# Gate, up and value products by token instead of by feature, and the last two down slabs of each network in token halves

## The reference

```python
def swiglu(h, w_gate, w_up, w_down):
    return (jax.nn.silu(h @ w_gate) * (h @ w_up)) @ w_down
...
for i in range(DEPTH):
    g = norm_gains[i]
    f = swiglu_2(rmsnorm_2(h, g[0]), ffn_gate[i, 0], ffn_up[i, 0], ffn_down[i, 0])
    h = h + MACARON * rmsnorm_2(f, g[1])
    mix = hybrid_mixer(rmsnorm_2(h, g[2]), cos_m, sin_m, cos_d, sin_d, w_in[i], q_norm[i], ...)
    h = h + rmsnorm_2(mix, g[3])
    f = swiglu_2(rmsnorm_2(h, g[4]), ffn_gate[i, 1], ffn_up[i, 1], ffn_down[i, 1])
    h = h + MACARON * rmsnorm_2(f, g[5])
    gate = jax.nn.sigmoid(rmsnorm_2(h, g[6]) @ w_ple_gate[i])
    h = h + rmsnorm_2((p[i].astype(h.dtype) @ w_ple[i]) * gate, g[7])
```

## Time and profile before

| | |
|---|---|
| median of 3 runs | 1837.92 us (1836.95 to 1840.16) |
| the profiled execution | 1842.03 us, its span 1840.4 us |
| mean granted TensorE clock | 0.973 |
| TensorE busy | 1734.6 us, 94% |
| weight loads | 1595.6 us, 87% |
| VectorE busy | 1216.6 us, 66% |
| ScalarE busy | 896.8 us, 49% |
| GpSimd busy | 122.2 us, 7% |
| chain that ended last | TensorE 78%, VectorE 11%, ScalarE 4% |
| transferred | 353.79 MB, 192 GB/s |

### The profile page before, as it was taken

The page is one execution under the profiler, slowest core; times in us unless marked ns, Lnnn a source line. Parts: engine busy times, 40 slices in busy tenths (PEclk is TensorE's granted clock), DMA queues, the critical chain, the costliest instruction groups (busy, mean ns, idle before and its releaser), DMA issues.

```text
span 1840.4 us, 29946 instructions
## 1 busy us (share of the span) xinstructions
PE 1734.6 (94%) x11826; PEld 1595.6 (87%) x11826; DVE 1216.6 (66%) x1599; ACT 896.8 (49%) x1235; POOL 122.2 (7%) x163
## 2 busy tenths in 40 slices
PE   6987899999899999999998999988999999999996
PEld 4986799989799998999896899978999896799986
DVE  7889787777765546555676665556655676765556
ACT  4572433356544335434476544345433557644345
POOL 2023111111010000000011000000000003000000
PEclk9998899999999999999999999998999999999999
DMA  9775598868345453555340555434555532355551
GB/s 380 280 292 182 209 358 315 308 232 312 144 172 206 182 183 134 199 193 189 136 178 10 184 200 187 177 138 148 196 193 182 172 138 69 126 184 185 180 197 42
DMA packets 61924, 353.79 MB, mean 192 GB/s; under 512 B 6522, under 2 KB 9738, under 8 KB 27792
## 3 DMA queue, kind: packets, MB, share of 16 engines
q1 hardware_dynamic: 40064, 281.24, 42.2%
q0 software_dynamic: 18384, 66.66, 10.1%
q10 hardware_dynamic: 3392, 4.72, 0.8%
HBM read 349.45 MB, written 3.15 MB: 192 GB/s over the span
## 4 chain that ended last, share of the span: by engine, by line
PE 78%; DVE 11%; ACT 4%; issue 3%; DMA 3%; POOL 0%; DVEq 0%; ACTq 0%; POOLq 0%
PE bank L528 23%; PE bank L529 23%; PE bank L530 23%; DVE w_lo L1509 2%; ACT w_hi L1021 2%; PE bank L560 1%; PE bank L562 1%; PE bank L561 1%; DMA shared<-in_mods 1%; PE bank L700 1%; DVE shared L1530 1%; PE bank L721 1%; DVE shared L2046 1%; PE bank L710 1%; DVE x L2055 1%
## 5 line engine op out<-in xcount | busy, mean ns | idle before, releaser
L528 PE MATMUL bank<-a_hi,w_hi 128*128 128x256 f32 x2648 | 758.8, 287 | 11.0 <-DVE a_lo L1577 3.6
L529 PE MATMUL bank<-a_lo,w_hi 128*128 128x256 f32 x2648 | 754.6, 285 | 0.0
L530 PE MATMUL bank<-a_hi,w_lo 128*128 128x256 f32 x2648 | 754.5, 285 | 0.0
L528 PEld LDWEIGHTS bank<-a_hi,w_hi 128*128 128x128 f32 x2648 | 513.9, 194 | 17.8 <-issue 11.5
L529 PEld LDWEIGHTS bank<-a_lo,w_hi 128*128 128x128 f32 x2648 | 514.0, 194 | 2.9 <-issue 0.7
L530 PEld LDWEIGHTS bank<-a_hi,w_lo 128*128 128x128 f32 x2648 | 513.5, 194 | 0.0
L1771 DVE TENSOR_TENSOR w_lo<-raw,w_hi 128x2048 fp32r<-128x2048 f32 x144 | 330.0, 2292 | 258.2 <-ACT w_hi L1162 258.2
L1162 ACT CAST w_hi<-raw 128x2048 fp32r<-128x2048 f32 x144 | 273.9, 1903 | 268.9 <-PE bank L530 268.9
L1509 DVE TENSOR_TENSOR w_lo<-raw,w_hi 128x2048 fp32r<-128x2048 f32 x119 | 272.1, 2292 | 133.5 <-ACT w_hi L1021 133.4
L1021 ACT CAST w_hi<-raw 128x2048 fp32r<-128x2048 f32 x122 | 231.3, 1907 | 90.9 <-PE bank L530 84.4
L528 PE MATMUL bank<-w_hi,hid_hi 128*128 128x512 f32 x548 | 215.8, 394 | 4.8 <-DVE hid_lo L2192 3.0
(11 more groups left out here) (242 smaller groups left out, 1948.8 us busy)
## 6 DMA issues: line engine op xcount, KB each, us to landing
raw<-in_stream SPq DMA_DIRECT2D x266, 1024.0 KB, 4.8
shared<-in_mods POOLq DMA_DIRECT2D x102, 512.0 KB, 6.3
grow<-in_rows POOLq DMA_DIRECT2D x12, 512.0 KB, 4.0
work<-in_mods POOLq DMA_DIRECT2D x8, 512.0 KB, 9.7
bias_rows<-work ACTq DMA_DIRECT2D x1, 2048.0 KB, 19.0
x<-in_x_t SPq DMA_DIRECT2D x1, 1024.0 KB, 6.2
x<-in_x_d ACTq DMA_DIRECT2D x1, 1024.0 KB, 4.9
work<-bias_rows ACTq DMA_DIRECT2D x1, 1024.0 KB, 10.5
```

The costliest lines, as they stand in the source:

```text
L528: pe.matmul(out, w_h, v_h, start=start, stop=False, skip_group_check=True)
L529: pe.matmul(out, w_h, v_l, start=False, stop=False, skip_group_check=True)
L530: return pe.matmul(out, w_l, v_h, start=False, stop=stop, skip_group_check=True)
```

## The change

- Gate and up columns of a group now lie side by side (512 columns), and a slab is half of the contraction (`split_rows`). `wide_slab` holds the activations of 128 tokens stationary and moves 512 weight columns. The output, by token, is gate and up of 256 features for 128 tokens in one bank. The dilated values, the shared values and the embedding gates have the same form.
- `hid` is now by token and is transposed on TensorE (`turn_hid`, four transposes a group) between the two halves of the next pair. ScalarE and VectorE read the transposed bank for `hid_hi` and `hid_lo`. The root mean square is now a scale per partition, so that the row for it and the separate scaling of gate and up are gone; `mean_row` is left for the mixers alone.
- The last two down slabs of a network run as (9, p0), the transposes of hid 10, (9, p1), (10, p0 and p1), (9, p2 and p3), (10, p2 and p3). The next stage begins with the first tokens (`first_tokens`), and `token_pair` transposes the second tokens' pieces within its second slab. `post`, `add_gated`, `turned_hi` and `turned_low` run in pieces of 128 tokens by four chunks, with the conversions of the next slabs between them.
- In FFN0 all four last modulation steps of VectorE stand ahead of the last `hidden`, and the reduction for the shared keys stands inside the last down slabs.
- In the mixer the value slabs come first, then the six others; in the shared keys and values too. Of the embedding, two gate slabs come first, then the embedding, then two gate slabs.

```diff
+            def wide_slab(slot, out, t, k, at=None, between={}):
+                for c in range(4):
+                    if at is not None:
+                        pe.wait_ge(nl_ready, at + CH * t + 4 * k + c + 1)
+                    mm = product(out[:, :], tokens(a_hi, 4 * k + c, t), tokens(a_lo, 4 * k + c, t), *weights(slot, 512 * c, 512),
+                                 start=(k == 0 and c == 0), stop=(k == 1 and c == 3))
+                    if c in between:
+                        between[c]()
                 return mm
...
+            def turn_piece(src, ready, p):
                 t, h = p // 2, p % 2
                 pe.wait_ge(*ready(p))
-                if free is not None:
-                    pe.wait_ge(*free)
-                for c in range(4 * h, 4 * h + 4):
-                    mm = pe.transpose(bank[4 + c // 2][:, (c % 2) * S + t * P:(c % 2) * S + (t + 1) * P],
-                                      src[:, t, c * P:(c + 1) * P], ident[:, :])
-                    if t == 1 and c % 2:
-                        mm.then_inc(turned, 1)
-            def turn_x(u, src, ready):
-                for p in range(4):
-                    turn_piece(src, ready, p, (f_ready, 4 * u + 4) if p == 1 else None)
+                for c in range(4):
+                    mm = pe.transpose(bank[4 + p][:, c * P:(c + 1) * P], src[:, t, (4 * h + c) * P:(4 * h + c + 1) * P], ident[:, :])
+                mm.then_inc(turned, 1)
+            def first_tokens(src, ready, warm=0, b=1):
+                keep_warm(warm, b)
+                for p in range(2):
+                    turn_piece(src, ready, p)
+            def token_pair(s, outs, at, src, ready):
+                need_slab(s)
+                wide_slab(s, outs[0], 0, 0, at)
+                need_slab(s + 1)
+                wide_slab(s + 1, outs[0], 0, 1, at, {1: lambda: turn_piece(src, ready, 2), 3: lambda: turn_piece(src, ready, 3)}).then_inc(half_done, 1)
+                wide_slab(s, outs[1], 1, 0, at).then_inc(slab_done, 1)
+                wide_slab(s + 1, outs[1], 1, 1, at).then_inc(slab_done, 1)
...
+                def first_half(done, slot, par, free=None):
+                    pe.wait_ge(lo_ready, done)
+                    if free is not None:
+                        pe.wait_ge(hl_ready, free)
+                    wide_slab(slot, bank[2 * par], 0, 0)
+                    wide_slab(slot, bank[2 * par + 1], 1, 0).then_inc(slab_done, 1)
+                def second_half(done, slot, par):
+                    pe.wait_ge(lo_ready, done)
+                    wide_slab(slot, bank[2 * par], 0, 1).then_inc(half_done, 1)
+                    wide_slab(slot, bank[2 * par + 1], 1, 1).then_inc(slab_done, 1)
+                def turn_hid(par, done):
+                    for t in range(2):
+                        pe.wait_ge(hid_done, done + (t + 1))
+                        for k in range(2):
+                            mm = pe.transpose(bank[2 * par][:, k * S + t * P:k * S + (t + 1) * P], hid[:, par, t * S + k * P:t * S + (k + 1) * P], ident[:, :])
+                        mm.then_inc(hid_turned, 1)
...
+                first_half(b + 3 * j, b + 3 * j - 1, 0, j - 1 + f0)
+                turn_hid(1, 2 * (f0 + j - 1))
+                second_half(b + 3 * j + 1, b + 3 * j, 0)
+                down(j - 1, b + 3 * j + 2, b + 3 * j + 1, 1, pieces=(0,))
+                turn_hid(0, 2 * (f0 + j))
+                down(j - 1, b + 3 * j + 2, b + 3 * j + 1, 1, pieces=(1,))
+                down(j, b + 3 * j + 3, b + 3 * j + 2, 0, last=True, pieces=(0, 1))
+                if i == 0:
+                    mod_reduce(G_KV, 3)
+                down(j - 1, b + 3 * j + 2, b + 3 * j + 1, 1, pieces=(2, 3)).then_inc(slab_done, 1)
+                down(j, b + 3 * j + 3, b + 3 * j + 2, 0, last=True, pieces=(2, 3)).then_inc(slab_done, 1)
...
-                need_slab(b + 1)
-                slab_pair((b, b + 1), (bank[0], bank[1]), before(APPLY_CHUNKS, apply2(l, LA_PREMIX)))
-                mean_row(4 * l + 1)
-                for i in range(2, 8):
-                    need_slab(b + i)
-                    if i in (4, 5, 6, 7):
+                token_pair(b, (bank[2], bank[3]), before(APPLY_CHUNKS, apply2(l, LA_PREMIX)), x, residual(u2(l, 0)))
+                mean_row(l)
+                for i in range(6):
+                    need_slab(b + 2 + i)
+                    if i in (2, 3):
+                        pe.wait_ge(qkv_act, c0 + i - 1)
+                    if i in (4, 5):
                         pe.wait_ge(qkv_dve, d0 + i - 3)
-                    if i < 6:
-                        mm = feature_slab(b + i, bank[i % 4])
-                    else:
-                        mm = token_slab(b + i, bank[i % 4])
-                    mm.then_inc(slab_done, 1)
+                    feature_slab(b + 2 + i, bank[i % 4]).then_inc(slab_done, 1)
+                    if i == 3:
+                        norm_stat(norm2(l, L_QLAT))
                     if i == 4:
-                        norm_stat(norm2(l, L_QLAT))
-                    if i == 5:
                         norm_stat(norm2(l, L_KVLAT))
...
+                post(u, 4 + 3 * l, b - 1, gain2(l, 2), b)
                 pre_squares(u)
                 c0, d0 = 8 + 8 * l, 6 * l
-                split_to(b + 3)
                 pre_rsqrt(4 * l + 1)
-                split_to(b + 4)
-                pre_row_copy(4 * l + 1)
-                def values(i):
-                    for t in range(2):
-                        ins = act.activation(v_dil[:, t, 256 * i:256 * (i + 1)], bank[2 + i][:, 256 * t:256 * (t + 1)], ACT.Copy,
-                                             scale=pre_r[:, t:t + 1])
-                    ins.then_inc(qkv_act, 1)
+                act.wait_ge(rpre_ready, 4 * l + 2)
+                act.wait_ge(rows_zero, 4)
+                for t in range(2):
+                    if t:
+                        act.wait_ge(slab_done, b + 2)
+                    else:
+                        act.wait_ge(half_done, halves_ffn(3 + 2 * l))
+                    act.activation(v_dil[:, t, :], bank[2 + t][:, :], ACT.Copy, scale=pre_r[:, t:t + 1]).then_inc(qkv_act, 1)
+                    split_to(b + 4)
+                pre_row_copy(l)
+                split_to(b + 5)
...
-                act.wait_ge(rows_zero, 4)
-                act.wait_ge(slab_done, b + 7)
-                act.wait_ge(rpre_ready, 4 * l + 2)
-                values(0)
-                act.wait_ge(slab_done, b + 8)
-                values(1)
...
-                made[0] = b + 3 * (FJ - 2) + 5
+                made[0] = b + 3 * FJ
                 j = FJ - 1
-                gate(j, j % 2, b + 3 * j)
-                split_to(b + 3 * j + 3)
-                hidden(j, j % 2, b + 3 * j + 1)
                 if i == 0:
                     mod(G_A1, 6)
-                split_to(b + 3 * j + 4)
-                hidden_lo(j, j % 2)
-                if i == 0:
                     mod(G_A1, 7)
-                split_to(b + 3 * j + 5)
+                hidden(j, 0)
+                split_to(b + 3 * FJ + 1)
+                hidden_lo(j, 0)
...
+                gained(0)
+                gained(1)
+                add(0)
+                gained(2)
+                turned_low(ap, 0, gain)
+                split_to(b + 2)
+                gained(3)
+                turned_low(ap, 1, gain)
+                add(1)
+                turned_low(ap, 2, gain)
+                turned_low(ap, 3, gain)
+                split_to(b + 3)
...
+                warm_up()
+                piece(0)
+                piece(1)
+                split_to(b + 2)
+                piece(2)
+                turned_hi(u, 0, gain)
+                piece(3)
+                for p in range(1, 4):
+                    turned_hi(u, p, gain)
+                split_to(b + 3)
...
+def split_rows(w):
+    yield wide(w[0:512])
+    yield wide(w[512:1024])
```

720 lines of the change are left out of this document (348 added, 372 removed).

## The result

| | before | changed |
|---|---|---|
| median of 4 runs each | 1839.04 us (1836.95 to 1843.09) | 1867.63 us (1862.3 to 1873.05) |
| profiled execution, its span | 1842.03, 1840.4 | 1862.3, 1860.6 |
| mean granted clock in it | 0.973 | 0.976 |
| TensorE busy | 1734.6, 94% | 1711.3, 92% |

The changed kernel takes 1.0146 times as long (95% interval 1.0120 to 1.0172): 27 us more by this ratio, 28.6 between the two medians. The forecast was 14 more, 1852 with a range from 1829 to 1868: the sign was right, the size was about half of what was measured. The profiled execution took 1862.3 against a forecast of 1856, the median is 1867.6 against 1852.

The account below looks back on a forecast made before the run. TensorE was taken to bound the kernel, busy 1734.6 of 1840.4 us. Gains of -20.8, new waits of +12.2 (FFN0) and +17.8 (mixers) and +5 for the clock gave +14: 1852 by the median, range 1829 to 1868.

Parts of the forecast that it names:

- FFN0's end: At FFN0's last hid, modulation steps awaiting transfers stand ahead of hidden: TensorE waits 10.1 us, hand-over +12.2, clock +2.
- mixers, with their clock: Ahead of the latent's up-projection, a small slab covers the rotated chain: 7.5 us wait, +8.9 per layer, clock +1.5 each.
- E + 3.2: 3.2 us after E, the end of a network's last gate/up product; at FFN0, when the loop's four modulation steps end.
- The wait at (10, p0): At a network's end, hid's low part stands behind the next slab's low part on VectorE: a new stall of 2.2 us.
- The clock term of +5: Granted clock falls after the new long waits: +2 us at FFN0, +1.5 per mixer; ends 0 and +15.
- Rival 3: At most hand-overs the clock falls, through short waits and transposes: +10 to +15 us, 1865; chance 0.15.
- I take -1.9 and -3.2: Bodies of the two modulated networks: no squares at the start, and idle TensorE the new order can hide.
- 31.9, so -0.85: Hand-over from the second network, one wait longer than the others: 31.9 us against 32.75.
- 1: The mixer's wait ahead of the up-projection does not appear, its chain having slack: 1831 us, faster; chance 0.2.
- 2: FFN0's wait is small, transfers being issued earlier, while the mixer's is there: 1842 us; chance 0.16.
- 4: In each step the wide product gains less or transposes cost more: 0.3 us per step, 66 steps, +20, 1872; chance 0.06.
- 5: VectorE's list decides, hand-overs stay as long as before and only the added waits remain: +17 us, 1869; chance 0.05.

Follow-up runs that it names:

- e10: Changed kernel with FFN0's last four modulation steps on VectorE moved from ahead of hidden to behind hid_lo; a single execution, 1860.3 us.
- e4: Changed kernel with the key latent's root and low part ahead of the mixer's last rotation, up-projection into free banks; median 1859.4 us, ratio 1.0122.
- e9: Changed kernel with 30 small filler matmuls, result unused, ahead of the wait for the key latent in the mixer; 1869.1 us.
- e3: Changed kernel with the last hid's high and low parts made ahead of the next slab's conversion; median 1857.6 us, ratio 1.0106.
- e13: Changed kernel unedited, profiled again; 1867.2 us at a mean granted clock of 0.973.
- e14: Changed kernel unedited, profiled once more; 1869.6 us at a mean granted clock of 0.970.
- e6: Changed kernel with the second network's rotary angle behind the slab conversion and hid_lo, and hid's high part ahead of the sine; median 1863.3 us.
- e11: Changed kernel with the last two down slabs in the old order, all pieces of one, then all of the other; 1850.2 us, ratio 1.0071.
- e15: Changed kernel without the ten filler matmuls after the second network; that hand-over took 43.90 us instead of 45.95.
- e16: Changed kernel with the edits of e10, e3, e4 and e6, without the filler after the second network; that hand-over took 41.93 us instead of 43.94.
- e12: Changed kernel with the edits of e10, e3, e4 and e6, and the last two down slabs in the old order; 1825.6 us, ratio 0.9943.

## Why the prediction was right or wrong

Forecast and measured, profile against profile, in us (measured: stages of the table above and of the earlier trace rows):

| term | forecast | measured |
|---|---|---|
| bodies of six networks | -5.1 | -4.8 |
| three hand-overs (mixers, FFN1's) | -4.85 | -1.9 |
| four after mixers and outputs | -10.4 | -8.6 |
| embedding, to the gates' end | +3.2 | +4.1 |
| behind the gates, and the last part | -3.6 | -4.2 |
| FFN0's end, with its clock | +14.2 | +14.4 |
| mixers, with their clock | +20.8 | +19.9 |
| the rest (start, shared keys to the output of MoBA) | 0 | +1.3 |
| sum | +14.25 | +20.2 |

**FFN0's end** was right in mechanism and nearly in size: one wait of 11.39 where 10.1 and, for the low part, 1.2 more were forecast; no second wait came. e10 confirms the order as the cause of 8.3 of it. The other 3.1 belong to the steps of the loop; the forecast's own times hold 2.5 of them (E + 3.2, hidden 0.7, TensorE due at E + 1.4) without giving them a name.

**The mixer** was right to 0.1 in the wait: 7.51 against 7.5, and 19.9 against 20.8 in both layers together. e4 shows half of the chain, e9 that the matmuls behind the wait are slow only because TensorE had idled.

**The wait at (10, p0)** was forecast at 2.2 and is 2.18, with its cause (e3).

**What failed.** Of the 15.6 us between 1852 and 1867.6, some 6 stand in the profile and 9.4 in the step from the profile to the median.

1. **The step to the median.** The old kernel's profiled execution lay 4.1 above the median of three (3.0 above that of four), and the forecast applied "the same difference" to the new one. The new kernel's first profile lies 5.3 below its median, and e13 and e14 show what it lacks: falls of the clock at hand-overs. The clock term of +5 fits the first profile, where FFN0's end and the mixers came out within 1 us of their sums; falls elsewhere, which the forecast put at nothing, are what a longer execution has more of. Rival 3 (1865, at 0.15) was this case in kind; the measured 1867.6 lies at the upper edge of the range.
2. **"I take -1.9 and -3.2"**: FFN1's body measured +1.0. I took idle time away and looked at no transfer there. The positions' transfer lands as late as before, and now stands ahead of a conversion too: 3.3 with its wait, and 1.6 more by a fall of the clock in that execution (e6, e11).
3. **"31.9, so -0.85"** for FFN1's hand-over: measured 34.31. Of these 2.4, 1.6 are a fall of the clock: in e14 the same code takes 32.75, at a clock of 1.00 instead of 0.95. The filler, of whose twenty records the walk had counted ten, is 0.4 to 0.5 (e15, e16); the cause of the last 0.4 is open.
4. **Luck in a sum.** Four bodies were 0.8 shorter each where I had 0, and FFN0's was 0.8 below its term: a step gains 0.17, not 0.12, and the start loses some 1.1, not 1.5. That the six bodies together came out at -4.8 against -5.1 is these errors cancelling that of FFN1.

**The rivals.** 1 and 2 (a stall that is not there) are refuted by the two waits. 4 is refuted by the step of 16.81, dense: a wide pair with its transposes gained 0.17. The same step speaks against the 32 us more, an estimate, that the isolated gap of the Trainium skill (TensorE: Matmul & The Clock Gate, "Back-to-back issue gap") would have made. 5, "the change does less than it says", I gave 0.05, and e11 and e12 show it for one part of the change: the halves gain 0.12 in a hand-over. My walk had the sign in it ("the first tokens' transposes wait for nothing") and did not ask how long they would wait with whole slabs: 0.28 in both kernels, so there was next to nothing to gain.

## What to carry to other kernels

When pieces are reordered so that one comes earlier, write down for each engine what stands ahead of its first use: here most losses were an operation with a late transfer, or a conversion, placed ahead of the one that TensorE waits for, and moving these alone turned 1.5% slower into 0.5% faster. Interleaving the last slabs delays the signal that frees the first of them, and whoever waits for that signal loses more than the halves bring. Compare forecasts with several profiles: one with few clock falls is not the median. And compare two kernels stage by stage only where the granted clock of the stage is the same: a fall of 1.6 us looked like the price of a filler here, and hid a gain of 2.1 around the embedding.

## What was not expected of the hardware

The same instructions in the same kernel take two lengths, 1.6 to 1.9 us apart, at a hand-over (31.76 or 33.34; 90.55 or 92.36), with a granted clock of 1.00 or 0.95 over the stretch; a filler of 6.9 us kept the matmuls behind it at full speed (1.70 against 2.93), and the execution as a whole was no shorter (a median of 1869.1 against 1867.6). A small matmul of float32 operands (128 columns, not in three parts) is two records of 0.11 us: 60 such took 13.5 us and 30 took 6.9.
